# Merging the row statistics of an attention step in the step after it, spread by DMA through DRAM

## What is computed

```python
m = jnp.max(s, axis=-1, keepdims=True)
p = jnp.exp(s - m)
den = jnp.sum(p, axis=-1, keepdims=True)
o = jnp.einsum('brnhqk,brnkhd->brnqhd', p, vc) / jnp.swapaxes(den, 3, 4)
lse = jnp.swapaxes((m + jnp.log(den))[..., 0], 3, 4)
...
wgt = jax.nn.softmax(jnp.stack(lses, axis=0), axis=0)
o_attn = jnp.sum(wgt[..., None] * jnp.stack(outs, axis=0), axis=0)
```

## Time and profile before

| | |
|---|---|
| median of 3 runs | 1835.39 us (1834.36 to 1835.42) |
| profiled execution | 1834.99 us, its span 1833.2 us |
| mean granted clock of TensorE | 0.992 |
| TensorE busy | 1788.0 us |
| VectorE busy | 1024.3 us |
| ScalarE busy | 561.8 us |
| GpSimd busy | 828.6 us |

### The profile page before, as it was taken

One profiled execution on the slowest core, in us unless ns is written; L12 is line 12 of the kernel. 1 busy time (PEld: TensorE's weight loads), 2 busy tenths in 40 slices (PEclk: granted clock), 3 DMA queues, 4 the chain that ended last, 5 costly groups with the idle time before them and its releaser, 6 DMA issues.

```text
span 1833.2 us, 23679 instructions
## 1 busy us (share of the span) xinstructions
PE 1788.0 (98%) x8628; PEld 1420.7 (77%) x8628; DVE 1024.3 (56%) x1545; ACT 561.8 (31%) x1069; POOL 828.6 (45%) x597
## 2 busy tenths in 40 slices
PE   8999999999999987999999999999999999999997
PEld 6777777777777766788888888788888888888786
DVE  6346645564655488343313323787787887644644
ACT  6533444354245423111411222533333333000000
POOL 7536443644544374554225734265455455222221
PEclk9999999999999999999999999999999999999999
DMA  4111111211121023445412244322232232345211
GB/s 173 36 41 47 52 53 41 64 52 41 41 58 47 24 70 93 112 114 132 144 64 70 92 141 169 138 82 90 69 93 79 69 103 92 137 150 194 81 54 49
DMA packets 64192, 158.08 MB, mean 86 GB/s; under 512 B 10912, under 2 KB 27680, under 8 KB 64112
## 3 DMA queue, kind: packets, MB, share of 16 engines
q1 hardware_dynamic: 51856, 145.35, 24.5%
q10 hardware_dynamic: 11792, 10.04, 1.9%
q0 software_dynamic: 464, 1.62, 0.2%
HBM read 123.54 MB, written 32.26 MB: 85 GB/s over the span
## 4 chain that ended last, share of the span: by engine, by line
PE 85%; DVE 8%; issue 3%; POOL 2%; DMA 1%; ACT 1%; SPq 0%; DVEq 0%; POOLq 0%
PE bank L911 13%; PE bank L912 13%; PE bank L913 13%; PE bank L1276 7%; PE bank L1278 7%; PE bank L1277 7%; PE bank L1334 4%; PE bank L1336 4%; PE bank L1335 4%; PE bank L925 2%; PE bank L1059 2%; PE bank L1072 2%; PE bank L1045 2%; DVE run_z L1774 1%; PE bank L1238 1%
## 5 line engine op out<-in xcount | busy, mean ns | idle before, releaser
L911 PE MATMUL bank<-hhi,whi 128*128 128x512 f32 x1024 | 421.0, 411 | 5.6 <-DVE hlo L1711 5.6
L912 PE MATMUL bank<-hlo,whi 128*128 128x512 f32 x1024 | 404.9, 395 | 0.0
L913 PE MATMUL bank<-hhi,wlo 128*128 128x512 f32 x1024 | 404.8, 395 | 0.0
L626 POOL TENSOR_TENSOR wlo<-raw,whi 128x1024 fp32r<-128x1024 f32 (+1 forms) x84 | 196.7, 2342 | 300.1 <-DVE whi L1667 298.1
L911 PEld LDWEIGHTS bank<-hhi,whi 128*128 128x128 f32 x1024 | 193.7, 189 | 52.5 <-issue 10.1
L913 PEld LDWEIGHTS bank<-hhi,wlo 128*128 128x128 f32 x1024 | 193.6, 189 | 45.4
L912 PEld LDWEIGHTS bank<-hlo,whi 128*128 128x128 f32 x1024 | 194.1, 190 | 39.5 <-issue 1.2
L1824 DVE CUSTOM_DVE_ANT_0 sp<-bank,mask 128x128 f32<-128x128 f32 (+1 forms) x192 | 56.3, 348 | 114.6 <-PE bank L1045 112.7
L1449 ACT ACTIVATE sp<-sp,negm 128x128 f32<-128x128 f32 (+1 forms) x192 | 83.9, 439 | 106.6 <-DVE negm L1828 106.5
L884 POOL TENSOR_TENSOR plo<-st,phi 128x512 fp32r<-128x512 f32 x60 | 79.5, 1328 | 58.6 <-ACT phi L1579 57.4
L2114 DVE CAST fhi<-ff 128x1024 fp32r (+1 forms) x44 | 31.4, 715 | 125.4 <-PE bank L1336 125.4
(11 more groups left out here) (304 smaller groups left out, 3927.8 us busy)
## 6 DMA issues: line engine op xcount, KB each, us to landing
raw<-in_wblocks SPq DMA_DIRECT2D x98, 512.0 KB, 3.6
pair<-in_wblocks SPq DMA_DIRECT2D x40, 512.0 KB, 4.8
ff_scr<-ffo SPq DMA_DIRECT2D x22, 512.0 KB, 5.9
ff<-ff_scr SPq DMA_DIRECT2D x22, 512.0 KB, 4.2
rt<-rt_scr SPq DMA_DIRECT2D x8, 516.0 KB, 6.6
x<-in_xT SPq DMA_DIRECT2D x8, 512.0 KB, 9.2
zb_scr<-zb SPq DMA_DIRECT2D x8, 512.0 KB, 3.3
zb<-zb_scr SPq DMA_DIRECT2D x8, 512.0 KB, 3.5
```

Source lines behind the costliest of these rows:

```text
L626: pool.tensor_tensor(wlo[par][:, 0:cols], raw[par][:, 0:cols], whi[par][:, 0:cols].bitcast(F32), ALU.subtract).then_inc(lo_done, 1)
L911: nc.tensor.matmul(ps, a, x, start=start and k == k_list[0], stop=False)
L912: nc.tensor.matmul(ps, a, y, start=False, stop=False)
L913: last = nc.tensor.matmul(ps, b, x, start=False, stop=stop and k == k_list[-1])
```

## The change

The statistics of steps 0 to 10 no longer go over `hx`, `rtmp` and sixteen transposes. `negm` and `den` are now one tile `sd` of 32 columns, ordered by head and block. In j = 9 TensorE transposes it once, into 32 rows of `b_nb`. In j = 10 ScalarE copies these to `st_t`. SP writes them to DRAM (`stat_scr`), waits for that, and reads them back with four DMAs, each spreading one row of 1024 values over 64 partitions: for pattern 0 straight into `run_n` and `run_z`, otherwise into the tile `bmd`, [P, 2, T] (`spread`; it stands between the weight loads on SP's queue).

The whole merge of a step moves to the slot after it: `merge_max` in j = 1 (h = 0) and j = 5 (h = 1), `merge_psum` and `merge_z` in j = 3 and 7, each behind the eviction of its sub-step. In slots with pattern 0 or 2 the weights' exponential stands first in j = 3 and 7 of ScalarE, ahead of the square; `rescale` and `weigh` are in j = 4 and 8 of POOL; the reciprocals are in j = 5 and 9 and `normalise` in j = 7 and 10 of the slots with pattern 0. `merge_max`, L1766 and `merge_z` now read only tiles in SBUF; the products L1765 still read a bank. For pattern 0, `run_n` and `run_z` need no copy. Step 11 merges in its own slot as before, from transposes.

```diff
+        stat_scr = nc.dram_tensor("stat_scr", [2, 2, T], F32).ap()
...
-            negm = sb("negm", [P, 8, 2])
-            den = sb("den", [P, 8, 2])
+            sd = sb("sd", [P, 2, 2, 8])
+            st_t = sb("st_t", [P, P])
             utmp = sb("utmp", [P, CH, NCH])
-            rtmp = sb("rtmp", [P, 2, GB, NCH // 2])
-            hx = sb("hx", [P, T])
+            bmd = sb("bmd", [P, 2, T])
...
-        stat = [hx[:], rtmp[:].rearrange("p a g k -> p (a g k)")]
+        negm, den = sd[:, 0], sd[:, 1]
+        stat = [bmd[:, h, :] for h in range(2)]
+        LAST = 3 * HP - 1
...
+            def spread(a, hp, ag):
+
+                sp_.wait_ge(st_copied, a + 1)
+                sp_.wait_ge(d_read, 2 * a + 1)
+                if ag == 0 and hp:
+                    sp_.wait_ge(o_ready, 2 * hp)
+                if a == 1:
+                    sp_.wait_ge(prep_b, 2)
+                sp_.dma_start(stat_scr.rearrange("i x (s q) -> (i x s) q", q=P), st_t[0:32, :]).then_inc(st_out, 16)
+                sp_.wait_ge(st_out, 16 * (a + 1))
+                for i, done in enumerate((sm_in, sz_in)):
+                    to = (run_n, run_z)[i][:, :] if ag == 0 else bmd[:, i, :]
+                    for x in range(2):
+                        sp_.dma_start(to[DH * x:DH * (x + 1)], stat_scr[i, x].unsqueeze(0).broadcast_to([DH, T])).then_inc(done, 16)
+
...
             for hp in range(HP - 1):
-                for b in range(10):
-                    load(B_ALOOP + 10 * hp + b, wblocks[B_ALOOP + 10 * hp + b], (b + 1) % 2)
+                for b in range(3):
+                    loop_load(hp, b)
+                if hp:
+                    spread(3 * hp - 1, hp - 1, 2)
+                for b in range(3, 6):
+                    loop_load(hp, b)
+                spread(3 * hp, hp, 0)
+                for b in range(6, 9):
+                    loop_load(hp, b)
+                spread(3 * hp + 1, hp, 1)
+                loop_load(hp, 9)
...
+            spread(LAST - 3, HP - 2, 2)
...
+            spread(LAST - 2, HP - 1, 0)
...
+            spread(LAST - 1, HP - 1, 1)
...
             def rescale(ag, hp, h):
                 nm = natural(num[:, :], ag, h)
+                if ag == 2:
+                    pool.wait_ge(merged, hpc(hp, 2) + 2)
                 pool.wait_ge(ab_exp, hpc(hp, ag) + h + 1)
                 chain.link(pool.tensor_tensor(nm, nm, split2(ab[h][:, 0, :], ag), ALU.mult))
...
-                    if a and ag == 0 and j == 0:
-                        weigh(a - 1, 2, hp - 1, 1)
-                    if a and ag == 0 and j == 5:
-                        normalise(2, hp - 1, 1)
+                    if a and ag != 1 and j in (4, 8):
+                        pg, ph, h = (ag + 2) % 3, hp - (ag == 0), j // 4 - 1
+                        rescale(pg, ph, h)
+                        weigh(a - 1, pg, ph, h)
+                    if a and ag == 0 and j in (7, 10):
+                        normalise(2, hp - 1, j == 10)
+                    if a and ag == 0 and j == 10:
                         pool.wait_ge(o_ready, 2 * hp)
                         pool.dma_start(o_scr[hp - 1], num[:]).then_inc(pool_dma, 16)
-                    if a is not None and ag > 0 and j in (10, 11):
+                    if g == 2 and j == 11 and hp < HP - 1:
+                        lo(b + 4, 0)
+                    if n is None and j in (10, 11):
                         h = j - 10
-                        if g == 2 and h and hp < HP - 1:
-                            lo(b + 4, 0)
                         rescale(ag, hp, h)
-                        if ag == 1 or n is None or h == 0:
-                            weigh(a, ag, hp, h)
-                        if ag == 2 and n is None:
-                            normalise(ag, hp, h)
-                        elif ag == 2 and h:
-                            normalise(ag, hp, 0)
+                        weigh(a, ag, hp, h)
+                        normalise(ag, hp, h)
...
-                                pe.wait_ge(m_read, 2 * a + 1)
+                                if a:
+                                    pe.wait_ge(st_copied, a)
...
-                    if a is not None and j in (9, 11):
+                    if n is None and j in (9, 11):
                         h = (j - 9) // 2
-                        pe.wait_ge(stat_done, 2 * a + h + 1)
+                        pe.wait_ge(stat_done, h + 1)
                         if h:
-                            pe.wait_ge(m_read, 2 * a + 2)
-                        elif n is not None:
-                            pe.wait_ge(ln_done, 4 * n + 4)
+                            pe.wait_ge(m_read, 1)
                         for s_ in range(4):
                             last = nc.tensor.transpose(b_nb[:, s_ * P:(s_ + 1) * P], stat[h][:, s_ * P:(s_ + 1) * P], ident)
                         last.then_inc(mt_done, 1)
-                    if a is not None and j in (10, 11):
+                    if n is None and j in (10, 11):
                         h = j - 10
                         if h:
                             pe.wait_ge(d_read, 2 * a + 2)
...
+                                if a and s_ % 4 == 0:
+                                    pe.wait_ge(d_read, 2 * a + s_ // 4)
...
-                            if s_ == 0:
-                                pe.wait_ge(d_read, 2 * a + 1)
-                            else:
+                            if a or s_:
...
+                        if n is not None and j == 9:
+                            pe.wait_ge(ln_done, 4 * n + 4)
+                            nc.tensor.transpose(b_nb[0:32, 0:P], sd[:].rearrange("p i x s -> p (i x s)"), ident).then_inc(mt_done, 1)
...
+            def weights_exp(ag, hp, h):
+
+                act.wait_ge(ab_in, 4 * hp + 2 * (ag - 1) + h + 1)
+                act.activation(ab[h][:], ab[h][:], ACT.Exp).then_inc(ab_exp, 1)
+
             def slot(n, g, b, a, ag, hp):
                 for j in range(12):
+                    if a and ag != 1 and j in (3, 7):
+                        weights_exp((ag + 2) % 3, hp - (ag == 0), j // 4)
                     if n is not None and j % 2 and j < 8:
...
-                    if a is not None and ag and j >= 10:
-                        h = j - 10
-                        act.wait_ge(ab_in, 4 * hp + 2 * (ag - 1) + h + 1)
-                        act.activation(ab[h][:], ab[h][:], ACT.Exp).then_inc(ab_exp, 1)
-                        if ag == NPAT - 1 and h:
+                    if a is not None and n is not None and j == 10:
+                        act.wait_ge(mt_done, a + 1)
+                        if a:
+                            act.wait_ge(st_out, 16 * a)
+                        act.activation(st_t[0:32, :], b_nb[0:32, 0:P], ACT.Copy).then_inc(st_copied, 1)
+                    if a and ag == 0 and j in (5, 9):
+                        reciprocal_z(hp - 1, NPAT - 1, j == 9)
+                    if n is None and j >= 10:
+                        weights_exp(ag, hp, j - 10)
+                        if j == 11:
                             reciprocal_z(hp, ag, 0)
-                    if a and ag == 0 and j == 3:
...
             def ublock(hp, n):
-                a = 3 * hp + 1
-                merge_psum(a, 1, hp, 1)
-                evict_u(hp, n, 0)
-                merge_z(a, 1, hp, 1)
-                evict_u(hp, n, 1)
+                for h in range(2):
+                    evict_u(hp, n, h)
...
             def merge_max(a, ag, hp, h):
-                dve.wait_ge(mt_done, 2 * a + h + 1)
-                nn, ps = natural(run_n[:, :], ag, h), split2(b_nb[:], ag)
                 if ag == 0:
-                    V.tensor_copy(nn, ps).then_inc(m_read, 1)
                     return
+                if a == LAST:
+                    dve.wait_ge(mt_done, LAST + h + 1)
+                else:
+                    dve.wait_ge(sm_in, 32 * (a + 1))
+                nn, new = natural(run_n[:, :], ag, h), split2(b_nb[:] if a == LAST else half(bmd[:, 0, :], h), ag)
                 down, up = (split2(ab[h][:, i, :], ag) for i in range(2))
                 if a == 1 and h == 0:
                     dve.wait_ge(prep_b, 2)
                 dve.wait_ge(merged, 4 * hp + 2 * (ag - 1) + h + 1)
-                dve.wait_ge(m_read, 2 * a + h + 1)
-                link(TT(up, nn, ps, ALU.subtract))
-                TT(nn, nn, ps, ALU.min).then_inc(m_read, 1)
+                link(TT(up, nn, new, ALU.subtract))
+                link(TT(nn, nn, new, ALU.min))
+                if a == LAST:
+                    dve.sem_inc(m_read, 1)
                 link(V.tensor_scalar(down, up, -1.0, 0.0, ALU.mult, ALU.min))
                 V.tensor_scalar(up, up, 0.0, None, ALU.min).then_inc(ab_in, 1)
 
             def merge_psum(a, ag, hp, h):
-                nm, nz = natural(num[:, :], ag, h), natural(run_z[:, :], ag, h)
                 dve.wait_ge(pv_done, 8 * a + 4 * h + 4)
-                dve.wait_ge(dt_done, 2 * a + h + 1)
+                if a == LAST:
```

(46 more changed lines are left out.)

10 lines of the change are left out of this document (6 added, 4 removed).

## The result

The changed kernel takes 1853.1 us (median; 1848.7 to 1856.7) against 1835.4 us: a ratio of 1.009, 95% interval 1.0076 to 1.0103. It is slower, and 5 us beyond the forecast of 1848.

A forecast was written before the change was run, and what follows sets the result against it. The prediction took TensorE, busy for 98% of the span, as the bound. It summed 1835.0 - 18.0 (transposes) + 2.7 + 7.8 (ordinary steps) + 20.5 (last step) = 1848 us, the forecast's own range 1840 to 1856.

The forecast's parts named there:

- Transposes: TensorE in steps 0 to 10: sixteen transposes go and one comes back, 1.64 us less per step, 18.0 us less.
- Transfers: Statistics sent over DRAM and back each step: 6 to 9 us per chain, taken as costing nothing, at most 1 us per step.
- The turns: Merge instructions newly reading SBUF (L1749, L1750, L1766 before the change) alternate with POOL, one whole instruction each.
- The sum by rows alone: Whole kernel: only instructions that took turns before do so now; last step +11, steps +10, 1839 us; chance 0.13.
- Ordinary steps: TensorE waits before the last step: +0.9 us in each of three merging pattern 2, +2.6 in three merging pattern 1.
- rival C: TensorE's idle stretches lower its clock, in the last step and after 2.4 us waits: another 8 to 20 us; chance 0.09.
- Last step: Two merges by turns with POOL, uncovered by matmuls: copies end at 56.2 us instead of 35.2, +20.5 us.
- After the last step: Rest of the kernel: taken as unchanged, with the last step's delay reaching the end of the kernel.
- Rival A: Whole kernel: turns cost little and odd sub-steps have room, so TensorE's saving stays; 1820 us, 1825 with half the stalls; chance 0.26.

The follow-up runs named there:

- x_hi_tr16: x_hi with sixteen transposes of constants put before the one new transpose in sub-step 9 of steps 0 to 10; 1857.5 us.
- x_hi_late: x_hi with SP writing the statistics to DRAM three times, a wait after each, before reading them back; 1838.5 us.
- x_tab: Changed kernel with POOL's nine table instructions moved from sub-steps 0 and 4 of the last slot to sub-step 11; 1855.1 us (one time).
- x_old10: Changed kernel with step 10 back on its old path: sixteen transposes and its merge where it was before; 1832.2 us.
- x_hi: Changed kernel with the rounding of weights in sub-step 1 of the ordinary slots moved behind `merge_max`; 1838.4 us.
- x_old10_hi: Changed kernel with the edits of x_old10 and x_hi together; 1820.2 us, 0.9916 of the kernel before.
- x_last: Changed kernel with the two weight roundings of the last slot moved behind each `merge_max` (sub-steps 0 to 1, 4 to 5); 1846.1 us.
- x_wexp: Changed kernel with the square put ahead of the weights' exponential on ScalarE in sub-steps 3 and 7; 1855.4 us.

## Why the prediction was right, and where its sizes were off

**Transposes, -18.0 us: right.** The steps without waits are 1.61 us shorter each, against the 1.64 of the forecast; for eleven steps that makes 17.7. x_hi_tr16 gives 0.108 us for a transpose, against 0.11.

**Transfers, nothing: right,** and shown by x_hi_late, with 4 us to spare.

**The turns: right, and the deciding choice.** The three instructions that had never waited with an operand in PSUM do wait with one in SBUF: L1797 has a median of 2.86 us, L1796 a maximum of 2.40 and L1816 one of 1.40. The sum by rows alone, without turns for them, was 1839. The Trainium skill's rule (SBUF — State Buffer, "SBUF: two separate sides") spoke against the change, and the trace of after agrees with it for all three.

**Ordinary steps, +10.5 us: the mechanism and nearly the size right, but the clock left out.** Steps that merge pattern 1 lost 2.6 us each, as forecast; those that merge pattern 2 lost 0.5 instead of 0.9. That makes 9.3 us. (The listed waits for the squares grew by 7.1 us, 12.4 for 5.3; some 0.7 us in each of steps 2, 5 and 8 stand under no listed wait.) What the forecast had at nothing was the clock. In the profile of after there are three stretches where the granted clock falls behind a wait of 2.27 us: the windows from 230 to 240 show 0.91 and 0.75, and others follow near 400 and 560. They cost 6.2 us. So rival C, at 0.09 and 8 to 20 us, was half true: its point (waits near 3 us) was already met at 2.3 us, beside waits that came out a little smaller than forecast. Which waits are followed by a fall differs from one profiled execution to another. That this also makes the spread of the changed kernel's times fits its mean granted clock, 0.983 in the execution of 1856.7 us and 0.987 in that of 1848.7: 0.004 of the span is 7.4 us, by estimate.

**Last step, +20.5 us: 20.4 measured,** by the mechanism given, but the match is partly luck. The copies start 49.5 us after the first matmul, where the forecast had 53, and end at 52.0 instead of 56.2. What follows them was forecast as unchanged and takes 20.7 us instead of 17.1. In the kernel before, the four copies took 7.4 us, so TensorE began the next matmuls beside the later ones; now they take 2.5, and these matmuls come after them and at the lower clock (one every 0.43 us instead of 0.23, until 698). The two errors, -4.2 and +3.6, nearly cancel. x_tab puts some 12 us of the growth on POOL's tables. x_old10 shows that the moved merge of step 10 is the cause: with it back in its old place, on its old operands, the copies end at 35.5.

**After the last step, nothing forecast, +3.8 measured.** The forecast took the rest of the kernel as unchanged. In x_hi the rest takes 1836.3 - 699.4 = 1136.9 us, 0.6 more than before; in x_hi_late, whose kernel is the same from there on, it takes 1140.1, as in after. So most of it differs from one profiled execution to another and is no fixed cost of the change; its cause was not tried.

Added up for the profiled execution: -17.7 for the transposes, +9.3 for waits and +6.2 for the clock in the ordinary steps, +20.4 in the last one, +3.8 behind it, and 0.4 less because step 0 began earlier, make the 21.7 to rounding. The forecast, 5 us short of the median, had the terms of the clock and of the rest at nothing.

Rival A failed on the last step and on L1797; but its number, 1820, is what the kernel gives when the two causes are taken out (x_old10_hi).

## What to carry to other kernels

Before moving VectorE work, ask of every instruction which operands lie in SBUF and what POOL runs beside it: an operand that moves from PSUM to SBUF can put a whole POOL instruction in front of each. An instruction that releases POOL (here a rounding of weights) belongs behind the VectorE work that must not wait, not ahead of it; but POOL work that stays in the stretch is only moved, and meets the next VectorE instructions. A merge cost 0.5 or 2.6 us, without the clock, in a step full of matmuls and 20 in the last one, which has few: look at the last turn of a pipeline by itself, and leave it on the old path if need be.

## What the runs showed of the hardware that was not expected

A wait of 2.27 us on TensorE, with matmuls before and behind it, can be followed by the lower level of its granted clock (1.2 GHz). It is not always: the three such waits of the changed kernel were, but only one of three in each of x_last, x_tab and x_old10. Where it fell, the two sums of squares behind the wait could take 1.89 us instead of 1.10, and the step was longer by 1.5 to 1.7 us, once by 3.0. Waits up to 1.5 us (the kernel before), 1.3 (x_wexp) and 0.6 (x_hi) were not followed by it in any ordinary step. TensorE in the changed kernel, and then behind the same wait in x_last:

```profile
233.94 1.89 PE L963 MATMUL bank<-sq,cst_s 128*128 128x512 f32 x2 [2.27 <-ACT sq L1432]
...
245.05 1.10 PE L963 MATMUL bank<-sq,cst_s 128*128 128x512 f32 x2
```

```profile
233.81 1.10 PE L963 MATMUL bank<-sq,cst_s 128*128 128x512 f32 x2 [2.27 <-ACT sq L1432]
```

Very small instructions take turns too: negating four maxima (L1880) has a median of 0.17 us in the changed kernel and took up to 1.64 us beside POOL.

The 16 KB written to DRAM landed after 1.4 us (median of 11), less than the 2.3 us taken from the earlier trace rows.
